# A ten-stage transformer kernel: norm factors of the mixers folded into later steps, rotations on one engine, mask and maximum in one operation

## What is computed

```python
def diff_attention(q, k, v, q_gain, k_gain, lam_vecs, out_gain, cos, sin, layer_idx):   # 8 heads x 2 maps x 64
    q = rotary_2(rmsnorm(q, q_gain), c, s_)
    k = rotary_2(rmsnorm(k, k_gain), c, s_)
    o = causal_block_attention(q, k, v, DIFF_HEAD_DIM ** -0.5)
    o = o[:, :, :, 0, :] - lam.astype(o.dtype) * o[:, :, :, 1, :]
    o = rmsnorm(o, out_gain) * (1.0 - lam_init)
def latent_attention(...):          # 8 heads x 96: q from a rank 384, keys and values from a rank 256
    q_rope = rotary_2(q_rope, cos[:, :, None, :], sin[:, :, None, :])
    q = rmsnorm(jnp.concatenate([q_nope, q_rope], axis=-1), q_gain)
    k = rmsnorm(jnp.concatenate([k_nope, k_rope], axis=-1), k_gain)
    o = causal_block_attention(q[:, :, :, None, :], k[:, :, :, None, :], v, MLA_QK_DIM ** -0.5)
def memory_cross_attention(...):    # 4 heads x 128 over 256 rows of a memory, not causal
    q = rmsnorm(q.reshape(B, S, CROSS_HEADS, CROSS_HEAD_DIM), q_gain)
    k = rmsnorm(kv[:, :, 0], k_gain)
merged = gates[:, :, 0] * y_diff + gates[:, :, 1] * y_mla + gates[:, :, 2] * y_mem
```

## Time and profile before

| | |
|---|---|
| median of 3 runs | 2763.22 us |
| profiled execution | 2763.35 us, span 2762.0 |
| PE busy | 2546.6 us, 92% |
| DVE, ACT, POOL busy | 1522.9, 1242.8, 591.3 us (55%, 45%, 21%) |
| chain that ended last | PE 74%, DVE 13%, ACT 5%, POOL 4%, issue 3%, DMA 1% |
| mean granted clock of PE | 0.952 of full |
| HBM | 415.28 MB read, 151 GB/s |

### The profile page before, as it was taken

How to read it: one execution, slowest core, us unless ns; L and a number is a source line. 1 busy time by engine, 2 the same in 40 slices (tenths; PEclk the granted TensorE clock), 3 DMA queues, 4 the chain that set the end, 5 groups by cost and what they waited for, 6 DMA issues and landing times.

```text
span 2762.0 us, 29805 instructions
## 1 busy us (share of the span) xinstructions
PE 2546.6 (92%) x11698; PEld 2054.1 (74%) x11698; DVE 1522.9 (55%) x1995; ACT 1242.8 (45%) x1894; POOL 591.3 (21%) x422
## 2 busy tenths in 40 slices
PE   7998999988998998999899877899999977999999
PEld 6886777766887887777787756777787855777787
DVE  4554444454555547555455565765554556765553
ACT  4444444434444445444444434445454433444543
POOL 1003222220000003422101454233100444223100
PEclk9999999878999999999999989999999988999999
DMA  6656545324655655444566543344566543334554
GB/s 218 180 179 181 167 131 152 95 56 140 182 183 165 180 181 174 145 145 140 170 180 188 167 130 106 86 123 145 168 184 190 171 118 101 99 115 139 166 172 149
DMA packets 213101, 418.38 MB, mean 151 GB/s; under 512 B 13728, under 2 KB 26928, under 8 KB 212961
## 3 DMA queue, kind: packets, MB, share of 16 engines
q1 hardware_dynamic: 204192, 388.55, 47.1%
q0 software_dynamic: 8336, 26.82, 3.2%
q10 hardware_dynamic: 432, 1.11, 0.1%
HBM read 415.28 MB, written 1.15 MB: 151 GB/s over the span
## 4 chain that ended last, share of the span: by engine, by line
PE 74%; DVE 13%; ACT 5%; POOL 4%; issue 3%; DMA 1%; ACTq 0%; DVEq 0%; POOLq 0%
PE banks L1321 21%; PE banks L1323 20%; PE banks L1322 20%; PE banks L1365 3%; ACT w_hi L1480 2%; PE banks L1415 2%; DVE w_lo L1720 2%; PE banks L1389 2%; PE banks L1400 2%; PE banks L1380 1%; POOL stat L2234 1%; ACT probs L1560 1%; POOL w_lo L2253 1%; DMA small<-in_diff_lambda 1%; DVE norm_sums L2090 1%
## 5 line engine op out<-in xcount | busy, mean ns | idle before, releaser
L1720 DVE TENSOR_TENSOR w_lo<-w_raw,w_hi 128x1024 fp32r<-128x1024 f32 (+1 forms) x594 | 742.6, 1251 | 924.2 <-ACT w_hi L1480 923.2
L1480 ACT ACTIVATE w_hi<-w_raw 128x1024 fp32r<-128x1024 f32 (+2 forms) x744 | 781.9, 1053 | 1025.8 <-PE banks L1323 977.6
L1321 PE MATMUL banks<-w_hi,xt_hi 128*128 128x512 f32 (+3 forms) x2112 | 850.0, 402 | 6.7 <-DVE xt_lo L1739 3.1
L1322 PE MATMUL banks<-w_lo,xt_hi 128*128 128x512 f32 (+3 forms) x2112 | 827.7, 392 | 0.0
L1323 PE MATMUL banks<-w_hi,xt_lo 128*128 128x512 f32 (+3 forms) x2112 | 827.0, 392 | 0.0
L2253 POOL TENSOR_TENSOR w_lo<-w_raw,w_hi 128x1024 fp32r<-128x1024 f32 (+2 forms) x150 | 359.0, 2395 | 580.9 <-ACT w_hi L1480 580.8
L1321 PEld LDWEIGHTS banks<-w_hi,xt_hi 128*128 128x128 f32 x2112 | 407.4, 193 | 95.6 <-DVE w_lo L1720 4.1
L1323 PEld LDWEIGHTS banks<-w_hi,xt_lo 128*128 128x128 f32 x2112 | 404.7, 192 | 90.0
L1322 PEld LDWEIGHTS banks<-w_lo,xt_hi 128*128 128x128 f32 x2112 | 406.5, 192 | 85.4 <-issue 3.1
L2234 POOL TENSOR_TENSOR stat<-stat,minus_half 128x1 f32<-128x1 f32 (+3 forms) x68 | 77.9, 1151 | 781.1 <-DVE stat L1790 615.6
L1321 PE MATMUL banks<-w_hi,ffn_ht_hi 128*128 128x512 f32 x352 | 141.6, 402 | 5.8 <-DVE w_lo L1720 5.8
(11 more groups left out here) (373 smaller groups left out, 3034.6 us busy)
## 6 DMA issues: line engine op xcount, KB each, us to landing
w_raw<-in_w_mlp SPq DMA_DIRECT2D x128, 512.0 KB, 3.7
w_raw<-in_w_in SPq DMA_DIRECT2D x104, 512.0 KB, 3.7
w_raw<-in_ffn_w_gate SPq DMA_DIRECT2D x88, 512.0 KB, 3.7
w_raw<-in_ffn_w_up SPq DMA_DIRECT2D x88, 512.0 KB, 3.7
w_raw<-in_ffn_w_down SPq DMA_DIRECT2D x88, 512.0 KB, 3.6
w_raw<-in_attn_w_in SPq DMA_DIRECT2D x72, 512.0 KB, 3.9
w_raw<-in_ret_w_in SPq DMA_DIRECT2D x64, 512.0 KB, 3.8
da_bias<-bias_by_distance POOLq DMA_DIRECT2D x48, 192.0 KB, 4.0
```

Of the source, the lines that this page charges most:

```text
L1321: pe.matmul(bank, xh, wh, start=(c == 0), stop=False)
L1322: pe.matmul(bank, xh, wl, start=False, stop=False)
L1480: act.activation(k.w_hi[i % SPLIT][:, 0:m], k.raw[i % RAW][:, 0:m], ACT.Copy).then_inc(*ev.mark(k.w_hi_made, ("w_hi", i)))
L1720: dve.tensor_tensor(lo, raw, hi.bitcast(F32), ALU.subtract).then_inc(*ev.mark(k.w_lo_made, ("w_lo", i)))
```

## The change

- **Rotations** of the mixers (`turning`) are six operations of DVE; POOL has no part in them. The tables of cos and sin for `mx_q` and `mx_k` are multiplied with the gains once per layer (`gained_tables`, eight operations of 128 x 64; the one for q with the sign turned).
- **Norm factors.** The factor of a row of q, xq or mq isn't multiplied in; it is kept in `head_scale` and used as the scale of the row in the softmax. `mx_k` and `mx_ck` are normed while they leave their bank (`bank_squares`, `bank_normed`), which keeps the bank until POOL has made the factor. `norm_gain` is gone; the gains of latent and cross attention (query and key multiplied together) and of the first attention's output are columns (`gain_columns`) that scale the copy out of a turn.
- **Mask and extreme in one pass.** `tensor_tensor_reduce` writes the masked, scaled and sign-turned scores and their minimum, once for each half of the rows, in all causal heads and in the dilated ones. The order shows it as ISA, with a second row for the read of its accumulator.
- **POOL's share** of `w_lo` in a mixer is 0 until attention starts, then 2 (110 tiles in all, where it was 150).
- **Order.** The preparing generators stand in another order; the four turns of the low-rank operand stand together after both halves' norms; `pause` may wait longer.
- Five of the ten broadcasts become loads of a column with one 4-byte number per partition, and stand behind the rest.

```diff
--- before.py
+++ after.py
...
-SMALL = dict(diff_q_gain_2=64, diff_k_gain_2=64, diff_out_gain_2=128, mla_qa_gain_2=384, mla_kva_gain_2=256,
-             mla_q_gain_2=96, mla_k_gain_2=96, cross_q_gain_2=128, cross_k_gain_2=128, diff_lambda_2=256)
+SMALL = dict(diff_q_gain_2=64, diff_k_gain_2=64, mla_qa_gain_2=384, mla_kva_gain_2=256, diff_lambda_2=256)
+COLUMNS = dict(mla_q_gain_2=96, mla_k_gain_2=96, cross_q_gain_2=128, cross_k_gain_2=128, diff_out_gain_2=128)
+COLUMN_AT = dict(mla_q_gain_2=0, mla_k_gain_2=1, cross_q_gain_2=2, cross_k_gain_2=3, diff_out_gain_2=4, mla=5, cross=6)
...
-    def pause(self, tiles, polls=8):
+    def pause(self, tiles, polls=16):
...
-            self.share = dict(dilated=3, retention=3, mix=2).get(kind, 0)
+            self.share = dict(dilated=3, retention=3).get(kind, 0)
...
-        self.step("norm_gain", n)
...
+    def leave_normed(self, b, dst, c0, d):
...
+            self.step("bank_squares", z)
+            zs.append(z)
+            yield
+        yield from self.pause(1)
+        for z in zs:
+            self.step("bank_normed", z)
+            yield
+        return [("evac", b.uid, half) for half in range(HALVES)]
...
+        self.step("gain_columns", layer)
+        yield
+        for n in range(2):
+            self.step("gained_tables", layer, n)
+            yield
...
-            got["k"] = yield from part("dk", k)
+            for c0, m in column_blocks(D):
+                got["k", c0] = yield from self.block(self.xt, w_in, D, IN_AT["dk"] + c0, m)
...
-        def diff_part(name, z, half, gain):
-            heads = z[:, half, :].rearrange("p (h d) -> p h d", d=DIFF_D)
-            t = yield from self.head_norm(heads, 2 * DIFF_H, DIFF_D, small(gain), got[name][half])
+        def diff_turned(name, z, half, tables, after):
+            heads, n = z[:, half, :].rearrange("p (h d) -> p h d", d=DIFF_D), DIFF_D // 2
+            four = [tables[:, i, half:half + 1, :].to_broadcast([P, 2 * DIFF_H, n]) for i in range(4)]
+            return self.turning(heads[:, :, 0:n], heads[:, :, n:], four, after + [("tables", layer, name)])
+
+        def diff_queries():
+            yield from need("q")
+            yield from together(*(diff_query(half) for half in range(HALVES)))
+            yield from turn_named("qt", lambda half, c: q[:, half, c * P:(c + 1) * P], qt, DC, got["q"][0] + got["q"][1])
+
+        def diff_query(half):
+            z = q[:, half, :].rearrange("p (h d) -> p h d", d=DIFF_D)
+            n = yield from self.head_rstd(z, 2 * DIFF_H, DIFF_D, got["q"][half], DIFF_D ** -0.5, self.head_scale[:, 1 - half, 0:2 * DIFF_H])
+            scaled["diff"].append(("norm_rstd", n.uid))
             yield
-            n = DIFF_D // 2
-            got[name][half] = [self.rotate(heads[:, :, 0:n], heads[:, :, n:], rope(0, half, 0, n, 2 * DIFF_H), rope(1, half, 0, n, 2 * DIFF_H),
-                                           [t, ("rope", 1)])]
+            got["q"][half] = [diff_turned("q", q, half, self.tables[0], got["q"][half] + [("squares", n.uid, h0) for h0 in (0, DIFF_H)])]
+
+        def diff_keys():
+            made = []
+            for c0, m in column_blocks(D):
+                yield from need(("k", c0))
+                made += yield from self.leave_normed(got["k", c0], k, c0, DIFF_D)
+            turned = []
+            for half in range(HALVES):
+                turned.append(diff_turned("k", k, half, self.tables[1], made))
+                yield
+            yield from turn_named("kt", lambda half, c: k[:, half, c * P:(c + 1) * P], kt, DC, turned)
...
+            self.share = 2
...
-                    self.turn(lambda h, c: o_diff[:, c, 1 - h, :], diff_t, half, [(c0 + c, c0 + c) for c in range(4)], [t], [got["diff", "vals"]])
+                    self.turn(lambda h, c: o_diff[:, c, 1 - h, :], diff_t, half, [(c0 + c, c0 + c) for c in range(4)], [t, ("gain_columns", layer)], [got["diff", "vals"]],
+                              gain=self.column("diff_out_gain_2", P))
...
-        prepared = together(diff_operand("q", q, qt, "diff_q_gain_2"), diff_operand("k", k, kt, "diff_k_gain_2"), memory_keys(), latent(), latent_keys(),
-                            cross_queries(), diff_outputs())
+        prepared = together(memory_keys(), diff_keys(), diff_queries(), latent(), latent_keys(), cross_queries(), diff_outputs())
...
-                    act.activation(p[:, row], bank[:, row], ACT.Exp, bias=h.nmax[:, s:s + 1], scale=h.scale, accum_out=h.den[:, s:s + 1]).then_inc(*done)
+                    act.activation(p[:, row], bank[:, row], ACT.Exp, bias=h.nmax[:, s:s + 1], scale=h.rows(s), accum_out=h.den[:, s:s + 1]).then_inc(*done)
...
-                pv = p[:, :].rearrange("p (s k) -> p s k", s=2)
-                done = ev.mark(k.dve_done, ("biased", h.uid), ("bank", "scores", h.uid))
-                if h.causal:
-                    n = h.keys(0) + h.keys(1)
-                    dve.scalar_tensor_tensor(p[:, 0:n], bank[:, 0:n], h.scale, h.bias, ALU.mult, ALU.add).then_inc(*done)
-                else:
+                if not h.causal:
                     q.wait_ge(*(yield from ev.of("bias", h.bias_no)))
-                    pair = bass.AP(h.bias.tensor, h.bias.offset, [list(h.bias.ap[0]), [P, 2], [1, SEQ]])
-                    dve.scalar_tensor_tensor(pv, view, h.scale, pair, ALU.mult, ALU.add).then_inc(*done)
+                for e in h.scaled:
+                    q.wait_ge(*(yield from ev.of(*e)))
+                for s in range(2):
+                    n = h.keys(s)
+                    at = s * SEQ if h.causal else s * P
+                    done = ev.mark(k.dve_done, *([("nmax_part", h.uid)] if s == 0 else [("nmax", h.uid), ("biased", h.uid), ("bank", "scores", h.uid)]))
+                    dve.tensor_tensor_reduce(p[:, s * SEQ:s * SEQ + n], bank[:, s * SEQ:s * SEQ + n], h.bias[:, at:at + n],
+                                             h.rows(s) if h.rows else -h.scale, BIG, ALU.add, ALU.min, h.nmax[:, s:s + 1]).then_inc(*done)
                 give_bank("scores", h.uid)
-                q.wait_ge(*(yield from ev.of("biased", h.uid)))
-                if h.causal:
-                    for s in range(2):
-                        done = ev.mark(k.dve_done, ("nmax_part", h.uid) if s == 0 else ("nmax", h.uid))
-                        dve.tensor_reduce(h.nmax[:, s:s + 1], pv[:, s, 0:h.keys(s)], AX.X, ALU.max, negate=True).then_inc(*done)
-                else:
-                    dve.tensor_reduce(h.nmax, pv, AX.X, ALU.max, negate=True).then_inc(*ev.mark(k.dve_done, ("nmax", h.uid)))
...
+        if what == "bank_normed":
...
+            q.wait_ge(*(yield from ev.of(*name)))
+            q.wait_ge(*(yield from ev.of("bank_rstd", z.uid)))
+            done = ev.mark(k.dve_done, ("evac", z.block.uid, z.half), ("bank", *name))
+            if z.block.scale:
+                q.wait_ge(*(yield from ev.of(*z.block.scale, z.half)))
+                dve.scalar_tensor_tensor(z.dst, view, k.row_scale[:, z.half:z.half + 1], r, ALU.mult, ALU.mult).then_inc(*done)
+            else:
+                dve.tensor_tensor(z.dst, view, r, ALU.mult).then_inc(*done)
+            give_bank(*name)
...
+        if what == "gained_tables":
+            layer, n = of
+            d = DIFF_D // 2
+            gain = k.small_of(("diff_q_gain_2", "diff_k_gain_2")[n])
...
+            for i in range(4):
+                side = (0, 1, 1, 0)[i]
+                g = gain[:, side * d:(side + 1) * d].rearrange("p (o d) -> p o d", o=1).to_broadcast([P, HALVES, d])
+                done = ev.mark(k.dve_done, ("tables", layer, "qk"[n]) if i == 3 else ("table", layer, n, i))
+                dve.scalar_tensor_tensor(k.tables[n][:, i, :, :], k.rope[:, i % 2, :, 0:d], (-1.0, 1.0)[n], g, ALU.mult, ALU.mult).then_inc(*done)
...
+            dve.tensor_tensor(one, second, second_sin, ALU.mult).then_inc(*ev.mark(k.dve_done, ("rot_second_sin", t.uid)))
+            dve.tensor_tensor(two, first, first_sin, ALU.mult).then_inc(*ev.mark(k.dve_done, ("rot_first_sin", t.uid)))
+            q.wait_ge(*(yield from ev.of("rot_first_sin", t.uid)))
+            dve.tensor_tensor(first, first, first_cos, ALU.mult).then_inc(*ev.mark(k.dve_done, ("rot_first_cos", t.uid)))
+            dve.tensor_tensor(second, second, second_cos, ALU.mult).then_inc(*ev.mark(k.dve_done, ("rot_second_cos", t.uid)))
+            q.wait_ge(*(yield from ev.of("rot_first_cos", t.uid)))
+            dve.tensor_tensor(first, first, one, ALU.subtract).then_inc(*ev.mark(k.dve_done, ("rot_first", t.uid)))
+            q.wait_ge(*(yield from ev.of("rot_second_cos", t.uid)))
```

219 lines of the change are left out of this document (165 added, 54 removed).

## The result

The changed kernel takes 2633.93 us (2632.53 to 2635.76, 4 runs) against 2762.58 for the kernel before in the same comparison: a ratio of 0.9538, 95% interval 0.9526 to 0.9549. It is 128.7 us faster.

What follows compares the result with a forecast made beforehand. TensorE (PE) was taken as the bound, so only its gaps and lower clock could be won. Terms 48.4 + 7.8 + 12.5 + 3.7 + 4 + 26 + 2 - 10 = 94.4 us off 2763.35 gave 2669; own range 2650 to 2690, with rivals 2637 to 2716.

Steps and rivals of the forecast that it cites:

- Term 1: Mixers' turns of q and k: rotations all on DVE finish just in time, removing PE's waits of 27.5 + 20.9, 48.4 us.
- Terms 3 and 4: Low-rank turns in the mixers: 12.5 us from waits and slow clock; ck, normed out of the bank in one pass: 3.7 us.
- Term 5: Prelude: fewer broadcasts ahead of the last small table shorten DVE's wait and PE's idling; 4 us, bounds -4 to 10.1.
- Term 8: Added work: DVE's extra w_lo queued behind bursts, k's banks held longer, table products; -10 us, between 0 and 40 lost.
- rival A: DVE becomes the bound in the preparing phase, bursts make w_lo late, heads give nothing; 2711 us, chance 0.17.
- Term 6: Mixers' heads: one-pass mask and minimum, fewer multiplies ahead; 21 us of waits plus 5 for clock, 26 us, bounds 5 and 47.
- Term 7: Dilated attention: one-pass operation changes nothing where PE runs at the lower clock; the few waits before shrink, 2 us.
- The clock terms: PE's slow-clock loss in the mixers: 7.8 us after q's and k's waits, 5 at low-rank turns, 5 at heads.
- Rival B: More is won: heads' waits vanish, 16 us more, and the last dilated group keeps full clock, 14 to 16; 2639, chance 0.12.
- C: One-pass operation is slow in 56 uncovered heads; gain gone at 2.1 us per 256 columns, 2787 us at 2.3; chance 0.05.
- D: Gap at q and k stays because something else in DVE's row is late, for instance the sums; 2706 us, chance 0.11.

Runs made afterwards that it cites:

- share_two: Changed kernel with POOL making every second w_lo in a mixer from its start, as before the change: ratio 0.9551 to the kernel before, 3.6 us slower than changed.
- rotation_and_share: Changed kernel with POOL making every second w_lo from a mixer's start and two operations of each rotation: ratio 0.9704 to the kernel before, 45.8 us slower than changed.
- rotation_on_pool: Changed kernel with two of six operations of each mixer rotation on POOL again: ratio 0.9623 to the kernel before, 23.5 us slower than changed.
- two_pass_mixers: Changed kernel with mask and minimum of the mixers' 48 causal heads in separate operations again: ratio 0.9586 to the kernel before, 13.3 us slower than changed.
- two_pass_dilated: Changed kernel with bias and maximum of the 48 dilated heads in separate operations again: ratio 0.9591 to the kernel before, 14.6 us slower than changed.
- all_three_back: Changed kernel with POOL's w_lo share, two operations per rotation on POOL, and q's norm and gain multiplies back: ratio 0.9718, 49.7 us slower than changed.
- k_norm_back: Changed kernel with k leaving its banks plainly, then normed and gain-multiplied in two passes per half: ratio 0.9566 to the kernel before, 7.7 us slower than changed.
- head_multiplies_back: Changed kernel with norm and gain multiplies for mq and xq, gain for kcat and attention output, back on DVE: ratio 0.9556, 5.0 us slower than changed.

## Why the prediction was too small

The forecast left 34.3 us out. By place, the terms for the mixers (1, 2, 3, 4, 6, 8) add up to 88.4 us, and 109.6 were measured; the dilated stage was to give 2 us and gave 11.7; all other stretches were to give 4 and gave some 7. Point by point, by its own steps:

- **Term 1 (q and k, 48.4 us)**: right. All of it is gone; a burst took 7.57 us (7.3 to 7.8 said), the margin was 1.1 us (1.1 said), and the turn was "just free". The reason given, operations of 2.8 and 3.4 us beside POOL, fits the trace before (8.1 us lost by them, against 5.6 us of waits for POOL). What the working left out is that the two go together: POOL's w_lo beside a rotation that doesn't wait for POOL costs little (share_two, 3.6 us, not told from none), and beside one that does it costs 22 us (rotation_and_share against rotation_on_pool).
- **Terms 3 and 4 (low-rank turns, ck)**: right; 7.5 and 3.7 us of waits are gone. No run undid them by themselves.
- **Term 5 (prelude)**: 4 taken, 5.8 found in the waits (10.1 to 4.3), within the bounds.
- **Term 8 (what is added)**: -10 taken. The new waits are 3.1 + 1.3 us, and no w_lo is late behind a burst. The step was oversized by about 6 us; I gave rival A's mechanism half its price though the working had shown that 7.8 us fit into 11.2.
- **Term 6 (heads)**: 21 us of waits taken, 24.6 found (42.4 to 17.8). The price of the one-pass operation was right: 0.9 us said, 0.76 to 0.99 measured. The pair's 0.48 + 0.35 us lies above the estimate of 0.39 + 0.26 from the Trainium skill ("VectorE: DVE Perf Modes", section "The TRN2 errata"). The halved throughput for two SBUF sources, of the Trainium skill's "Vector Engine (DVE) Microarchitecture Reference", section "Points that are easy to get wrong", isn't seen with one source in PSUM. The one-pass operation takes 0.479 us for 256 columns, and the mask alone, without a minimum, takes 0.478 in two_pass_mixers:

```profile
L1956 DVE SCALAR_TENSOR_TENSOR probs<-banks,head_scale,causal 128x256 f32<-128x256 f32 x48 | 22.9, 478 | 12.0 <-PE banks L1480 12.0
```

- **Term 7 (dilated, 2 us)** is the step that failed, by 9.7 us. It says that a faster DVE changes nothing at the lower clock level, and that only the few waits before it shrink. It looked at the long slow stretch (slice 540 to 560 in the earlier trace rows, still at 0.50), and not at the heads after it, where PE fell to the lower level again behind waits of 1.65 and 2.52 us. The stage gave 11.7 us: 3.9 of waits, 7.7 of PE's busy time. two_pass_dilated gives it back.
- **The clock in the mixers** is the second: its mechanism was right and its size 11 us short. The clock terms were 7.8 + 5 + 5 = 17.8 us, all in the mixers; PE's busy time fell by 28.8 there and by 39.0 in all. The waits add up to 27.5 + 20.9 + 24.6 + 7.5 + 0.7 + 3.7 - 4.4 = 80.5 us (0.7 is one more wait in front of a turn of `tok`), near the 80.8 of idle time. By slices of 4 us, an estimate, the loss went from 29.6 to 5.6 us: 9.6 of it at q and k (7.8 taken), 8.0 from the heads on (5 taken), 6.4 ahead of q, where the low-rank turns lie (5 taken). So no single place was missed here; each was somewhat short, and some 5 us of the 28.8 aren't placed by the slices.

Rival B had this direction (heads' waits all gone and the last dilated group at full clock, 2639), but not this mechanism: neither happened. The heads kept 17.8 us of waits, and the last group kept its 0.50. Its sum takes 16 us for the waits that were left, though 42.4 less the 21 taken leaves 21; with these its time would have been near 2633, the measured one, by luck and not by its reasons. The forecast's own range is also a little off: half of each way to the bounds of terms 6 and 8 gives 2653 to 2694, not 2650 to 2690. A, C and D are refuted by the rows above. What the parts are worth, undone one at a time: all_three_back 49.7, two_pass_dilated 14.6, two_pass_mixers 13.3, k_norm_back 7.7, head_multiplies_back 5.0, in all 90.3 of about 128 us. This is a rough sum: parts cost more together than alone, two_pass_mixers made a head dearer than it had been, and the two smallest are near their intervals. The rest was not tried: the order and merging of the turns, the low-rank turns and ck (11.9 us of waits), and the prelude's loads (5.8). Of these, the order is the largest open rival for a part of term 1: with all three edits PE waits 9.7 and 5.0 us at q and k, where it waited 13.8 and 10.4.

## What to carry to other kernels

When PE's waits shrink, read its clock level beside each of them, also the short ones: here 90 us less of waits came with 39 us less of busy time for the same work, and a wait of 1.02 instead of 1.65 us (1.69 instead of 3.04 with its neighbours) was followed by the full level instead of the lower one. A handshake between engines costs what is queued ahead of it on the other engine, and an experiment in the new order can put something else there than the old order had (two powers of 5.9 us here): compare the waits with the trace of before, ahead of saying what the old stall was. Where a margin has been worked out to be there, price the added work at its margin and not at half its worst case.

## What the hardware showed that was not expected

- The read of the one-pass operation's accumulator (0.08 us) starts together with the next pass (both at 1646.22), so it costs nothing there.
- The minimum comes free with the mask: 0.479 us with it, 0.478 without (256 columns, a factor for each row).
- The one-pass operation is dearer with a factor for each row than with a constant: 128x256 took 0.479 us in the mixers (mean of 48, a row factor from SBUF) and 0.421 in the dilated heads (mean of 66, a constant; the row below, by form). The mask of the kernel before agrees: 0.549 us for 384 columns with a constant, where 0.61 is what the two passes with a row factor (0.479 and 0.347) lead to, an estimate:

```profile
L1956 DVE CUSTOM_DVE_ANT_0 probs<-banks,da_bias 128x256 f32<-128x256 f32 x66 | 25.2, 421 | 31.4 <-PE banks L1480 31.4
```

- POOL's power of 128x16 numbers takes 2.9 us (5.78 for two), longer than its w_lo of 128x1024 (2.41).
